# HG levels of a two-block layer stack: upper-half columns of each block instead of all 128 per chunk

## The reference, cut to what matters

```python
def step(S, inp):
    qi, ki, vi, gi = inp
    b = jnp.cumsum(gi, axis=2)
    diff = b[:, :, :, None, :] - b[:, :, None, :, :]
    decay = jnp.where(causal, jnp.exp(jnp.where(causal, diff, 0.0)), 0.0)
    scores = jnp.einsum('bhtk,bhtsk,bhsk->bhts', qi, decay, ki)
    o = (jnp.einsum('bhts,bhsv->bhtv', scores, vi)
         + jnp.einsum('bhtk,bhkv->bhtv', qi * jnp.exp(b), S))
```

## Time and profile before

| | before |
|---|---|
| median of three runs | 2173.45 us |
| the profiled execution, its own time | 2173.69 us |
| its span in the trace | 2171.9 us |
| TensorE busy | 1917.3 us, 88% |
| VectorE busy | 1011.8 us, 47% |
| ScalarE busy | 865.7 us, 40% |
| GpSimd busy | 601.4 us, 28% |
| mean granted TensorE clock | 0.956 |

### The profile page before, as it was taken

The page is one execution under the profiler, slowest core; times in us unless marked ns, Lnnn a source line. Parts: engine busy times, 40 slices in busy tenths (PEclk is TensorE's granted clock), DMA queues, the critical chain, the costliest instruction groups (busy, mean ns, idle before and its releaser), DMA issues.

```text
span 2171.9 us, 35369 instructions
## 1 busy us (share of the span) xinstructions
PE 1917.3 (88%) x14368; PEld 1530.4 (70%) x14368; DVE 1011.8 (47%) x1327; ACT 865.7 (40%) x1236; POOL 601.4 (28%) x255
## 2 busy tenths in 40 slices
PE   4999988899997996988899998799687999998987
PEld 3777877699775684877798765666565886777755
DVE  7576376632535046375632635847605224132232
ACT  2333455533523333456433524256524332233332
POOL 1343432300242343422300331321232441322312
PEclk9899999999998898999999998899899999999999
DMA  8662222200423121222200423211133221211111
GB/s 325 215 223 68 80 90 82 68 4 4 171 91 111 62 95 58 88 82 72 69 4 18 170 87 145 78 59 39 43 117 112 97 97 39 78 55 62 59 66 71
DMA packets 60826, 192.89 MB, mean 89 GB/s; under 512 B 5632, under 2 KB 5888, under 8 KB 60320
## 3 DMA queue, kind: packets, MB, share of 16 engines
q1 hardware_dynamic: 60704, 191.10, 25.5%
HBM read 173.25 MB, written 17.83 MB: 88 GB/s over the span
## 4 chain that ended last, share of the span: by engine, by line
issue 57%; PE 24%; POOL 11%; DVE 4%; ACT 3%; POOLq 0%; DVEq 0%; ACTq 0%
PE proj L1910 13%; POOL w_lo_sb L702 10%; PE aux L2120 3%; PE aux L2051 2%; DVE area_sb L1253 2%; PE aux L2177 1%; PE proj L2120 1%; PE aux L2174 1%; ACT L798 1%; DVE area_sb L1256 0%; ACT L905 0%; PE aux L2107 0%; PE aux L1952 0%; PE aux L1941 0%; PE aux L2029 0%
## 5 line engine op out<-in xcount | busy, mean ns | idle before, releaser
L702 POOL TENSOR_TENSOR w_lo_sb<-w_raw_sb,w_hi_sb 128x1024 fp32r<-128x1024 f32 x231 | 583.2, 2525 | 1361.6 <-ACT w_hi_sb L778 1361.6
L1910 PE MATMUL proj<-act_hi_sb,w_hi_sb 128*128 128x512 f32 x1480 | 604.6, 409 | 66.2 <-POOL w_lo_sb L702 49.3
L1910 PE MATMUL proj<-act_lo_sb,w_hi_sb 128*128 128x512 f32 x1480 | 584.4, 395 | 0.0
L1910 PE MATMUL proj<-act_hi_sb,w_lo_sb 128*128 128x512 f32 x1480 | 584.3, 395 | 0.0
L778 ACT ACTIVATE w_hi_sb<-w_raw_sb 128x1024 fp32r<-128x1024 f32 x231 | 244.3, 1058 | 737.1 <-PE proj L1910 521.7
L1910 PEld LDWEIGHTS proj<-act_hi_sb,w_hi_sb 128*128 128x128 f32 x1480 | 283.2, 191 | 140.0 <-POOL w_lo_sb L702 46.1
L1910 PEld LDWEIGHTS proj<-act_lo_sb,w_hi_sb 128*128 128x128 f32 x1480 | 283.2, 191 | 62.7 <-issue 6.7
L1910 PEld LDWEIGHTS proj<-act_hi_sb,w_lo_sb 128*128 128x128 f32 x1480 | 282.7, 191 | 60.9
L1930 PE MATMUL aux<-act_hi_sb,w_hi_sb 128*128 128x512 f32 x336 | 139.0, 414 | 57.8 <-issue 43.2
L1253 DVE TENSOR_TENSOR area_sb<-area_sb 128x256 f32<-128x256 f32 (+2 forms) x208 | 141.5, 719 | 19.9 <-ACT area_sb L930 11.8
L1930 PE MATMUL aux<-act_lo_sb,w_hi_sb 128*128 128x512 f32 x336 | 136.2, 405 | 0.0
(11 more groups left out here) (255 smaller groups left out, 2565.6 us busy)
## 6 DMA issues: line engine op xcount, KB each, us to landing
w_raw_sb<-wall SPq DMA_DIRECT2D x231, 512.0 KB, 3.2
area_sb<-w_ada SPq DMA_DIRECT2D x32, 512.0 KB, 4.8
slots_sb<-w_ada SPq DMA_DIRECT2D x16, 512.0 KB, 8.3
gate_scr<-stage_sb SPq DMA_DIRECT2D x32, 256.0 KB, 2.2
area_sb<-gate_scr SPq DMA_DIRECT2D x8, 1024.0 KB, 9.5
x_scr<-area_sb SPq DMA_DIRECT2D x3, 2048.0 KB, 7.4
area_sb<-x_scr SPq DMA_DIRECT2D x3, 2048.0 KB, 9.7
area_sb<-lru_gates SPq DMA_DIRECT2D x1, 3584.0 KB, 11.7
```

The source lines that it names most:

```text
L702: nc.gpsimd.tensor_tensor(w_lo[:, b % 2, :, :].rearrange("p k n -> p (k n)"), w_raw[:, b % 2, :], w_hi[:, b % 2, :, :].rearrange("p k n -> ...
L1910: ins = MM(bank, w[:, s, k, :], a[:, t, :], start=(start and i == 0), stop=(stop and i == len(terms) - 1))
```

## The change

TensorE streams only the upper-half columns of each block of the level, 64 of 128 per chunk, into the columns of the product where they belong; the other columns of the bank are not written. VectorE copies only these columns. The stationary operand is still the whole 128 x 128 slot. At level n the columns come in runs of m = 2^(n-1): single columns with a step of two at level 1, runs of two at level 2, and one run of 64 per chunk at level 7. The number of instructions, their order and their waits are the same.

```diff
+        def upper(ap, m):
+
+            return ap.rearrange("p (c b h m) -> p c b h m", c=ap.shape[1] // P, h=2, m=m)[:, :, :, 1, :]
+
         def halves(ap, m):
...
                         dve.sem_inc(S("level_landed"), 1)
-                        mask = spread(C("hgmask", P * n, P), 4).bitcast(I32)
-                        job_read(nc.vector.copy_predicated(in_chunks(scores, P), mask,
-                                                           in_chunks(aux[bank][:, :], P)), ("level", l, n))
+                        m = 1 << (n - 1)
+                        mask = halves(C("hgmask", P * n, P), m)[1].unsqueeze(1)\
+                            .to_broadcast([P, 4, P // (2 * m), m]).bitcast(I32)
+                        job_read(nc.vector.copy_predicated(upper(scores, m), mask, upper(aux[bank][:, :], m)),
+                                 ("level", l, n))
...
                                 r = ring[(n - 1) % 3][:, cols]
-                                ins = MM(x[:, cols], r, r, start=True, stop=True)
+                                m = 1 << (n - 1)
+                                ins = MM(halves(x[:, cols], m)[1], r, halves(r, m)[1], start=True, stop=True)
```

## The result

The changed kernel takes 2180.22 us (median of six runs, 2174.86 to 2182.43) beside 2172.16 us for the kernel before: a ratio of 1.0035, with an interval of 1.0025 to 1.0045. It is slower, by an interval clear of no change. The forecast was no change, 2172.3, in a range that ended at 2180; the median lies 0.22 us above it, and slower by over 0.2% had been given 0.16.

A forecast was written before the change was run, and what follows sets the result against it. TensorE, busy for 88% of the span, was taken to bound the kernel; 8 turns x 0.16 = 1.3 us off 2173.69 (2172.4) and off the median 2173.45 (2172.2) gave 2172.3 us, range 2166 to 2180.

The forecast's parts named there:

- the weight given to the clock: TensorE around the wait between levels 4 and 5: half columns could halve the clock each turn, 14 us, 2187; 6%.
- TensorE's pitch: Level matmuls: weight loads set 0.111 us a pair, so 64 columns save 0 a level, bounds 0 and 0.44 us.
- Rival 2: Level matmuls: pitch follows the columns, 0.44 us for each of levels 2, 5, 6, 7; 14 us, 2160; 8%.
- VectorE's copies: Seven copies a turn on VectorE: 512 to 256 elements, 730 to 440 ns, 0.29 us less each.
- The prediction's upper bound of 1.02 us: VectorE's copies: length if each element took twice its 290 / 256 ns and the rest stayed.
- rival 3: Copies 1 and 2 over 0.80 us each let GpSimd in before level 6's difference; 5 us slower, 2179; 9%.
- The 0.16 us a turn: Level 6's difference, GpSimd and level 5 move forward: 323.37 instead of 323.53, 0.16 us a turn.
- GpSimd's run ahead of level 5: GpSimd's subtraction before level 5: about 2.6 instead of 2.79 us, as a sign that the forecast is right.
- the 0.04 us between the end of level 3 and the difference for level 6: VectorE's difference waits for level 3's ring slot: some 0.04 us until level 3's end is seen.
- Before levels 6 and 7 TensorE waits for nothing: TensorE's run of levels 6 and 7: no wait before it, so copies 4 to 7 are not asked for.
- The sum itself, 1.3 us less: Both HG loops: 8 turns x 0.16 = 1.3 us less.
- Rival 5: Level matmuls: stepped PSUM writes at four times a column's time, 0.82 us more a level; 26 us, 2199; 4%.

The follow-up runs named there:

- the two covered kernels: Kernel before with half copies and gate pieces moved one place forward, before levels 5 and 6; levels at 128 or 64 columns: ratios 0.9967 and 0.9970.
- the copies alone: VectorE copies only the upper columns, TensorE streams all 128 columns as in the kernel before: ratio 0.9995 to that kernel.
- full levels 4 and 5: The whole change, but levels 4 and 5 stream all 128 columns: ratio 0.9995 to the kernel before.

## Why the prediction was wrong

**The step that failed** is the weight given to the clock: "Levels 4 and 5 and the wait between them, at half the columns, could bring it on in each turn: 14 us, 2187. Against it: the loop holds 1.00 over its waits, and the loads and gates stay. 6%." The place and the cause were as written there. The argument against it was not one. That the clock holds over a wait with full levels on both sides says nothing of the margin, and the rows at hand spoke the other way: over products of one column matmuls and weight loads were both busy for all of 4.20 us, and the clock stood at 0.50, so neither kept it up there. The sum priced the columns at nothing because the weight load hides them, and did not ask what else they gave. The size was over: 14 us assumed a fall in each turn of 1.7 us. Measured in the profiled execution were five of eight, two of 1.5 us, two of 4.6 or 4.7 and one that the ends of the turns don't separate, less the 3.2 that came back between the loops.

**TensorE's pitch** was right. One column, 64 and 128 all give 0.111 to 0.112 us per pair, by the one-column row and by the run of 1.00 us above; the two covered kernels, 64 and 128 columns at the same time, show it without the clock. Rival 2 was out. The table of section "Back-to-back issue gap" in the Trainium skill's "TensorE: Matmul & The Clock Gate" is given there for single matmuls, and at 0.112 us for 64 columns and for 128 it is no rule for this stream, which loads weights for each matmul.

**VectorE's copies** were mis-sized in two of seven. They take 0.43 us in runs of 4 and more, as taken, but 0.72 in runs of 1 and 2, hardly less than the 0.73 for twice the elements (kernel after, copies 2 and 3 of that turn):

```profile
322.85 0.72 DVE L1523 COPY_PREDICATED area_sb<-const_sb,aux 128x256 f32<-128x256 int32 x1
...
324.77 0.43 DVE L1523 COPY_PREDICATED area_sb<-const_sb,aux 128x256 f32<-128x256 int32 x1
```

(5 x 0.43 + 2 x 0.72) / 7 = 0.51, the group's mean. The prediction's upper bound of 1.02 us was summed wrongly: twice 290 / 256 ns for each of 256 elements adds 0.29 to 0.44, which is 0.73 and what copies 1 and 2 took. Since they did not grow past 0.80 us, the change of order of rival 3 did not come. (Its own terms, 326.0 + 0.2 + 0.6 + 0.3 to 0.6 + 0.7, put level 5 at 327.8 to 328.1 and not at 327.6 to 327.9.)

**The 0.16 us a turn** came out as 0.15, but by luck, since two thirds of it came from another place. GpSimd's run ahead of level 5 fell only from 2.79 to 2.73 us:

```profile
324.35 2.73 POOL L702 TENSOR_TENSOR w_lo_sb<-w_raw_sb,w_hi_sb 128x1024 fp32r<-128x1024 f32 x1 [5.07 <-ACT w_hi_sb L782]
```

With the copies alone it did not fall (2.78). The term that was mis-sized is the 0.04 us between the end of level 3 and the difference for level 6, which overwrites its slot. It is 0.15 us in all three kernels: 323.53 against 322.33 + 1.05 before, 324.17 against 323.02 + 1.00 after, and 324.13 against 322.93 + 1.05 with the copies alone:

```profile
322.93 1.05 PE L2057 MATMUL aux<-area_sb 128*128 128x128 f32 x8
...
324.13 0.69 DVE L1257 TENSOR_TENSOR area_sb<-area_sb 128x512 f32 x1
...
324.27 2.78 POOL L702 TENSOR_TENSOR w_lo_sb<-w_raw_sb,w_hi_sb 128x1024 fp32r<-128x1024 f32 x1 [5.06 <-ACT w_hi_sb L782]
```

So the difference hung on level 3 in the kernel before already. Shorter copies 1 and 2 could not have moved it, and only the 0.05 us of level 3's shorter last record was left.

The other 0.1 was in the run of levels 6 and 7, which went from 2.04 to 1.95 us with the copies alone and 1.89 with the shorter last record. Fifteen steps of 0.112 and a last record of 0.275 make 1.95, so the old run held a wait of 0.1 us: level 7 needs the bank that copy 5 reads. In the kernel before copy 5 ends at 329.55 + 0.72 = 330.27, and level 7's first weight load starts at 330.39, where the pitch would have put it at 330.28:

```profile
329.55 0.72 DVE L1517 COPY_PREDICATED area_sb<-const_sb,aux 128x512 f32<-128x512 int32 x1
...
330.39 0.30 PEld L2051 LDWEIGHTS aux<-area_sb 128*128 128x128 f32 x2
```

"Before levels 6 and 7 TensorE waits for nothing" was true of level 6; the merged row hid level 7. The run in the timeline of the kernel with the copies alone:

```profile
330.10 1.95 PE L2057 MATMUL aux<-area_sb 128*128 128x128 f32 x16
```

The sum itself, 1.3 us less, fits the kernels that have no falls: 0.9995 for copies only and for full levels 4 and 5, which is 1.1 us, though neither interval excludes no change.

**Rival 5** was out. Level 1 writes single columns with a step of two and takes 1.00 us for 8, as level 3 does with runs of four. The Trainium skill's rule in "PSUM — Partial Sum Buffer", section "Specifications (TRN2)", that a pattern which isn't contiguous slows matmuls, does not show at the pitch that the weight loads set; a matmul without them wasn't tried.

**What stays open.** Why the clock falls in five turns of eight and not in all or none, and why it stays at half for some 3 us in one and 10 in another, no run here says, nor why the wait of 1.29 us before level 2, which has gate matmuls in front of it, brought no fall in any kernel. The times after the change spread from 2174.86 us (mean granted clock 0.955) to 2182.43 (0.950, the profiled one). How many falls the other executions had isn't on record.

## What to carry to other kernels

Here columns that hid under a weight load cost no time, and taking them away brought TensorE's clock down. Before taking such columns away, look for a wait before or behind the thinned matmuls, and look at the granted clock in windows of the same turn, not at its mean (0.95 after, 0.956 before). Where a stretch is thin, cover the wait with work that is due anyway, here a gate piece moved one place, or stream something useless in it, which here won the loss back and no more. Read a merged row of many matmuls against count times pitch, since a small wait inside it is not marked.

## What the runs showed of the hardware that I had not expected

- The clock fell just behind a wait of only 1.45 to 1.52 us, when at least one of the levels beside it (some 1 us each) streamed 64 instead of 128 columns: in 23 of 40 turns of the five kernels profiled. With 128 on both sides it held in all 24 turns of the three kernels that have this wait (1.40 to 1.47 us).
- Level matmuls of 128 and of 64 columns look alike in TensorE's busy share: they start 0.112 us apart, and TensorE is busy for 88% of the span in both kernels. What the missing columns did shows in the granted clock alone.
- A predicated copy of 256 float32 elements out of PSUM takes 0.72 us in runs of 1 and of 2 elements, and 0.43 in runs of 4 to 64. Multiplies in SBUF with runs of one take 0.42 us in both kernels.
